# Last mixers of a two-block layer stack: the next head's masked maximum ahead of the division

## The reference, cut to what matters

```python
o_a = moba_attention(qa, ka, va)          # 8 heads of width 64; 256 tokens are one block,
                                          # so this is causal softmax attention over it
o_h = hgrn2_chunkwise(...)                # gated recurrence, 4 heads of 128
o_m = memory_attention(qm, km, vm)        # 4 heads of width 128, no mask, over 256 memory rows
y = concatenate([o_a, o_h, o_m], axis=-1) * silu(z)
x = x + y @ w_out[l]
```

## Time and profile before

| | |
|---|---|
| median of 3 executions | 1626.62 us |
| the three | 1626.62, 1626.62, 1623.18 us |
| the profiled execution | 1630.73 us |
| its span, first to last instruction | 1628.8 us |
| mean granted clock of TensorE, share of full | 0.968 |
| busy: PE, PEld, DVE, ACT, POOL | 1552.1, 1380.3, 1177.2, 769.3, 94.3 us |
| chain that ended last | PE 78%, DVE 13%, ACT 6%, issue 3% |

### The profile page before, as it was taken

One profiled execution on the slowest core, in us unless ns is written; L12 is line 12 of the kernel. 1 busy time (PEld: TensorE's weight loads), 2 busy tenths in 40 slices (PEclk: granted clock), 3 DMA queues, 4 the chain that ended last, 5 costly groups with the idle time before them and its releaser, 6 DMA issues.

```text
span 1628.8 us, 23944 instructions
## 1 busy us (share of the span) xinstructions
PE 1552.1 (95%) x9974; PEld 1380.3 (85%) x9974; DVE 1177.2 (72%) x1391; ACT 769.3 (47%) x943; POOL 94.3 (6%) x66
## 2 busy tenths in 40 slices
PE   7999998998999999999998999999999899899998
PEld 6888898887888888888987888888999579799757
DVE  7888667636887788786676787867787565589644
ACT  5433545325433454335535534355656554554643
POOL 1000000010000000000000100001031001012000
PEclk9999989999999999999999999999999799999969
DMA  7555533204555545555421555544543124434202
GB/s 275 194 197 181 180 128 132 78 27 160 202 186 185 184 174 193 195 181 181 181 104 68 214 184 186 192 169 151 181 156 119 63 104 168 144 130 148 86 1 78
DMA packets 51888, 246.76 MB, mean 151 GB/s; under 512 B 4619, under 2 KB 5771, under 8 KB 27718
## 3 DMA queue, kind: packets, MB, share of 16 engines
q1 hardware_dynamic: 50662, 238.29, 41.2%
q0 software_dynamic: 1120, 6.96, 1.2%
HBM read 244.18 MB, written 1.05 MB: 151 GB/s over the span
## 4 chain that ended last, share of the span: by engine, by line
PE 78%; DVE 13%; ACT 6%; issue 3%; DMA 0%; SPq 0%; DVEq 0%; POOL 0%; ACTq 0%
PE ps L1055 19%; PE ps L1057 10%; PE ps L1006 9%; PE ps L1007 9%; PE ps L1008 9%; PE ps L1107 7%; PE ps L1252 4%; PE ps L1108 4%; DVE w_lo L1814 3%; ACT w_hi L1499 2%; DVE act_two L1920 1%; PE ps L1367 1%; PE ps L1396 1%; PE ps L1411 1%; ACT act_two L1577 1%
## 5 line engine op out<-in xcount | busy, mean ns | idle before, releaser
L1499 ACT ACTIVATE w_hi<-raw 128x2048 fp32r<-128x2048 f32 x188 | 359.2, 1914 | 390.3 <-PE ps L1057 278.3
L1814 DVE TENSOR_TENSOR w_lo<-raw,w_hi 128x2048 fp32r<-128x2048 f32 x188 | 437.2, 2331 | 144.4 <-ACT w_hi L1499 141.4
L1055 PE MATMUL ps<-act_two,w_hi 128*128 128x512 f32 x1408 | 445.1, 398 | 5.0 <-DVE w_lo L1814 2.4
L1006 PE MATMUL ps<-act_two,w_hi 128*128 128x256 f32 x1120 | 329.7, 294 | 16.8 <-DVE act_two L1920 5.4
L1007 PE MATMUL ps<-act_two,w_hi 128*128 128x256 f32 x1120 | 320.2, 286 | 0.0
L1008 PE MATMUL ps<-act_two,w_lo 128*128 128x256 f32 x1120 | 320.2, 286 | 0.0
L1057 PEld LDWEIGHTS ps<-act_two,w_lo 128*128 128x128 f32 x1408 | 265.9, 189 | 63.1
L1057 PE MATMUL ps<-act_two,w_lo 128*128 128x256 f32 x1408 | 277.8, 279 | 0.0
L1006 PEld LDWEIGHTS ps<-act_two,w_hi 128*128 128x128 f32 x1120 | 218.3, 195 | 23.5 <-issue 7.8
L1055 PEld LDWEIGHTS ps<-act_two,w_hi 128*128 128x128 f32 x1408 | 215.4, 189 | 8.0 <-DVE w_lo L1814 3.6
L1007 PEld LDWEIGHTS ps<-act_two,w_hi 128*128 128x128 f32 x1120 | 218.3, 195 | 3.2 <-issue 3.1
(11 more groups left out here) (282 smaller groups left out, 2079.0 us busy)
## 6 DMA issues: line engine op xcount, KB each, us to landing
raw<-panels SPq DMA_DIRECT2D x184, 1024.0 KB, 4.8
raw<-panels SPq DMA_DIRECT2D x80, 512.0 KB, 4.8
raw<-panels SPq DMA_DIRECT2D x8, 256.0 KB, 5.7
table<-tab POOLq DMA_DIRECT2D x1, 1472.0 KB, 9.4
table<-tab POOLq DMA_DIRECT2D x1, 1216.0 KB, 5.5
xn<-x_in SPq DMA_DIRECT2D x4, 256.0 KB, 4.8
work<-mem_in POOLq DMA_DIRECT2D x1, 1024.0 KB, 9.3
xn<-mem_in POOLq DMA_DIRECT2D x1, 1024.0 KB, 5.2
```

The source lines that it names most:

```text
L1006: pe.matmul(o, l[0], r[0], start=start, stop=False, skip_group_check=shared)
L1055: pe.matmul(grid(ps[:, bank + half], 2), w[half][0], act_two[:, slots[c]], start=c == 0, stop=False)
L1499: nc.scalar.activation(w_hi[:, s], raw[:, s], ACT.Copy).then_inc(panel_hi, 1)
L1814: tt(w_lo[:, s], raw[:, s], w_hi[:, s].bitcast(F32), ALU.subtract).then_inc(panel_lo, 1)
```

## The change

One word: the rounds of the heads in the two last mixers take ATTEND_TWO in place of ATTEND.

```diff
--- before.py
+++ after.py
@@ -397,7 +397,7 @@
               [[]] * n + rounds(NORM_COLS, qk + [(f"ho{l}", 0), (f"ho{l}", 1), (f"sq{l}", 0), (f"sq{l}", 1)]),
               [[]] * (n + 2) + rounds(ROPE, qk),
               [[]] * (h + 11) + [[("dve", "gate_out", ((f"moba{l}", g),)) for g in (0, 1)]],
-              [[]] * h + rounds(ATTEND, [(f"moba{l}", i) for i in range(8)] + [(f"matt{l}", i) for i in range(4)]),
+              [[]] * h + rounds(ATTEND_TWO, [(f"moba{l}", i) for i in range(8)] + [(f"matt{l}", i) for i in range(4)]),
               [[]] * (h + 13) + [y_splits(l, 0), y_splits(l, 2)]]
```

## The result

The changed kernel takes 1635.81 us in the median of 7 runs (1631.72 to 1637.36), the kernel before 1626.62 on the same chip (7 runs, 1621.64 to 1627.66). The ratio is 1.0062 with a 95% interval of 1.0047 to 1.0077: slower by 9.2 us between the medians, 10.1 by the ratio, 7.6 to 12.5 by its interval. The profiled execution of after took 1634.24 us.

The account below looks back on a forecast made before the run. PE bounds moba rounds (3.88 us, lower clock); masked maximum, exponential and division bound memory attention (2.90). Losses of 4.6 us in layer 0 and 3.5 in layer 1 sum to 8.1, taking 1626.62 to 1634.7 us; range 1630 to 1640.

Parts of the forecast that it names:

- The loop: Moba rounds, lower clock: division, turn, scores, masked maximum, next division form a 4.15 us loop, where PE alone needs 3.88.
- The start: Start of each layer's heads: masked maximum goes first, so the first division and first turn come 0.74 us later.
- Heads of memory attention: Layer 0, turn of head 6 to masked maximum of head 11: 12.48 us instead of 11.50, a loss of 0.98.
- The gating: Layer 0's last stretch: gating (1.42 us) now runs beside turn and scores, giving about 1.5 us back.
- Layer 0: Heads of layer 0: loses 3.62 us to the turn of head 6 and 0.98 after, 4.6 us in all.
- Layer 1: Heads of layer 1: loses 0.74 us at the start, 1.87 in six rounds and 0.88 after, 3.5 in all.
- the clock's return: Heads of memory attention: a round earlier saves layer 0 0.8 us; a round later costs 1.2 us more per layer.
- The upper bound: Top of the total loss's stated bounds, 5 to 11.5 us, for what the rows don't fix.
- the one `scale`: Layer 0, round 6: shifted memory-norm order costed at nothing; if its cover is gone, one `scale`, 0.75 us.
- Rival 1: Memory attention heads: clock stays low two rounds more in both layers, 4.9 us on top, 1639.6 us; chance 0.15.
- Rival 2: Heads' rounds: exponential overlaps the division, bounded by the larger of PE and DVE; 2 us gained per layer, 1622.6; chance 0.05.
- Rival 3: Heads: moba rounds swallow the division, norms and gating cover the rest; plus 1 us or so, 1627.6; chance 0.09.

Follow-up runs that it names:

- The last edit: ACT's six second-memory-norm steps one per round, added to new DVE order, scores first on PE and seven useless products: 1609.11 us, 0.9901 of the kernel before.
- the kernel with the products and both old orders: Kernel before plus seven useless PE products in the pause ahead of each last mixer's first division: 1620.37 us, ratio 0.9967.

## Why the prediction was right

**The loop.** As forecast: division, turn, scores, masked maximum, division, held together by PE's order. 4.09 us where 4.15 was worked out; the 0.06 are the step from the masked maximum to the division, 0.67 instead of 0.74, since the price came from a row in which the norm's `scale` stood behind it. To the turn of head 6 layer 0 lost 0.68 at the start and 2.55 in the rounds, 3.23 against 3.62.

**The start.** 0.68 us for 0.74, and taken away alone by the kernel with the old first round (0.66).

**Heads of memory attention**, in layer 0. 4.18, 3.22 (1311.04 to 1314.26), 3.32 and 1.64 us for 4.35, 3.20, 3.31 and 1.62, together 12.36 for 12.48. The gating gave back its 1.5 us as said.

**Layer 0**: 4.1 us for 4.6, all of it handed on to the start of layer 1.

**Layer 1**: the mis-sized term, and the one that varies. The rounds at the lower clock are as forecast (4.10, 4.57, 4.25, 4.58 for 4.31, 4.58, 4.31, 4.58; the first is 4.36 and not 4.15, with 0.27 us more between the two parts of its masked maximum, and the second none of the `turn_back` that I charged to it). But the clock came back one round earlier than forecast: from the turn of head 5 it took 3.47 us for 4.31, from that of head 6 3.14 for 4.35. So 1.3 us in this profile for 3.5. It is the bound that the prediction named, the clock's return, only that it put one round at 0.8 us in layer 0; here one round gave back 2.0, and other profiles of layer 1 show several rounds. The profiles of layer 1 range from 32.25 to 37.61 us for one and the same order. The 1.3 and the forecast 3.5 both start from before's late return (37.61); with an early clock in both kernels layer 1 lost 4.3.

**The total, and how much of it was luck.** +9.2 and +7.3 us between the medians agree with the sum of 8.1. The parts don't: layer 0 alone has 0.9 and 2.4 us (2.3 and 2.4 by the ratio) for 4.6, layer 1 alone 5.1 (5.7) for 3.5. The rounds, the start and the handing on are the mechanism as it was forecast, and the profiles show them; that two misses of about 2 us, both of the size that the clock makes, cancel in the sum was luck. The upper bound was not worked out either: the named terms give 5.1 us at the least, as stated, but 10.5 at the most (11.3 with the one `scale`), not 11.5.

**Rival 1**, clock low for longer: in layer 1 not in the pair of profiles, where it came up earlier. Over the timed runs it isn't refuted: layer 1 only has a mean clock of 0.9708 against 0.9731 for before beside it, and it costs more than the profiles show at like clocks (5.7 us by the ratio, against 4.3). In layer 0 it came up a little later in time (0.60 for 0.75 in the window 1305 to 1310) but, as before, with the scores of head 8. **Rival 2**, the overlap: false for this change, true once PE's order is turned and the clock is up. **Rival 3**, no matter: false, by both groups of runs.

Open: what decides in which round the clock returns in layer 1. Of the nine profiles without the added products it came three rounds early or more in five, one round early in the changed kernel's two, and late in two (the kernel before, and the new DVE order with the scores first). Whether a later start of the layer, or the order of DVE, has a part in it is open. Nor is all the spread between executions there: the work ahead of the first changed instruction, the same in all these kernels, ended anywhere between 1276.92 and 1282.02 us in the nine profiles. The last edit, ACT's steps one a round, was not run without the others.

## What to carry over

Before a step is moved ahead on one engine, follow what that step's input waits for on the engine that makes it: if an in-order queue there puts it behind the very result that was moved back, the two steps no longer overlap but close a loop. Sum the loop and set it against the busiest engine's round; here 4.09 against 3.88, and two steps exchanged in the other engine's queue took the scores out of it. And ask what else holds the round at its length: here a lower clock hid both the gain of the overlap and a 3.3 us stall on ACT, and edits that bring 0.3% at best where they were run alone, and a loss in the case of this one, bring 1.0% together with one that was not.

## What the runs showed of the hardware

Being busy was not enough to leave the lower clock. In the moba rounds of layer 0 of before PE was busy for 20 us on end at a granted clock of 0.50, while in layer 1 of the kernel with the products and both old orders it was busy less, at full clock (the same window view, before and then that kernel):

```profile
1287.00:1297.00 10.00, 10.00 (x28) 5.69 (x29) 3.99 (x20) 4.20 (x15) 0.00 (x0) 0.50 0.00 0
1297.00:1307.00 10.00, 10.00 (x30) 5.96 (x29) 4.31 (x18) 7.77 (x28) 0.00 (x0) 0.50 0.00 1
...
1550.00:1555.00 5.00, 4.60 (x27) 2.97 (x26) 2.53 (x15) 3.44 (x11) 0.00 (x0) 1.00 0.00 0
```

The same order of layer 1 got its clock back in one execution at about 1562 and in another at about 1577, 14.7 and 28.9 us behind its L2065, which is 5.4 us of 1626: it is more than the change costs in a layer, so one profile of each kernel can't tell that cost. The mean clock of each timed run, at 0.9 us per 0.001, says how far the clock has a part in a difference, but a change that lengthens a stretch at the lower clock moves it too.
